# Weight splits one per slot, input rows split in two portions, sample values and large copies asked for at other times

## The reference

```
u = rmsnorm(x) @ w_in                       # 1024 -> 10256 columns
o_a, state = gla(q, k, v, log_a, state0)    # gated linear attention, 4 heads
for window, dilation in ((128, 1), (512, 4), (2048, 16)):
    o_g, lse_g, new_cache_g = dilated_attention(q_g, k_g, v_g)
o_b = softmax(lse) weighted sum of o_g
merged = sigmoid(ga) * ((norm(o_a) * silu(gg)) @ w_gla_branch) + sigmoid(gb) * ((o_b * silu(dg)) @ w_dil_branch)
h = x + rmsnorm(merged @ w_out)
y = h + (pe @ w_ple_proj) * sigmoid(h @ w_ple_gate)
```

## Time and profile before

| | us |
|---|---|
| median of 3 runs | 2909.12 (2906.79 to 2913.81) |
| the profiled execution | 2904.35 |
| its span | 2902.2 |
| PE busy | 2659.9 (92%) |
| DVE, ACT, POOL busy | 1673.6, 1031.6, 806.6 |
| granted clock of PE, mean | 0.962 |

### The profile page before, as it was taken

One profiled execution on the slowest core, in us unless ns is written; L12 is line 12 of the kernel. 1 busy time (PEld: TensorE's weight loads), 2 busy tenths in 40 slices (PEclk: granted clock), 3 DMA queues, 4 the chain that ended last, 5 costly groups with the idle time before them and its releaser, 6 DMA issues. The chain is left out here.

```text
span 2902.2 us, 54195 instructions
## 1 busy us (share of the span) xinstructions
PE 2659.9 (92%) x21916; PEld 2045.2 (70%) x21916; DVE 1673.6 (58%) x3025; ACT 1031.6 (36%) x1880; POOL 806.6 (28%) x805
## 2 busy tenths in 40 slices
PE   4778989998979999899999987999999999999998
PEld 3667867776867778788998886997887544444444
DVE  6455766654544565556666654667655565554552
ACT  4222544322211222223334443544433344444441
POOL 5234322432333444333325322332222000000000
PEclk8899999999989999999999998999999999999999
DMA  5588766978787788768758676544435976666552
GB/s 155 124 255 276 262 220 219 326 261 275 245 266 243 247 246 299 276 225 287 239 174 295 212 247 235 186 155 140 139 133 201 316 198 157 173 168 165 167 115 56
DMA packets 370057, 622.38 MB, mean 214 GB/s; under 512 B 199196, under 2 KB 204899, under 8 KB 365330
## 3 DMA queue, kind: packets, MB, share of 16 engines
q1 hardware_dynamic: 311554, 352.11, 39.3%
q0 software_dynamic: 44000, 233.26, 24.4%
q10 hardware_dynamic: 14256, 33.56, 3.2%
HBM read 429.15 MB, written 244.66 MB: 232 GB/s over the span
## 5 line engine op out<-in xcount | busy, mean ns | idle before, releaser
L832 PE MATMUL out<-w_hi,x_hi 128*128 128x256 f16 x3136 | 868.3, 277 | 52.8 <-DVE stage L750 28.6
L832 PE MATMUL out<-w_lo,x_hi 128*128 128x256 f16 x3136 | 867.6, 277 | 0.0
L832 PE MATMUL out<-w_hi,x_lo 128*128 128x256 f16 x3136 | 867.0, 276 | 0.0
L750 DVE SCALAR_TENSOR_TENSOR stage<-out,stage 128x512 f32<-128x512 f32 (+1 forms) x567 | 378.5, 680 | 408.8 <-PE out L832 291.7
L684 DVE SCALAR_TENSOR_TENSOR w_lo<-raw,w_hi 128x1024 f16<-128x1024 f32 x280 | 403.2, 1455 | 19.0 <-ACT w_hi L680 18.4
L830 PE MATMUL out<-x_hi,w_hi 128*128 128x256 f16 x1344 | 372.8, 277 | 31.0 <-ACT stage L738 13.9
L680 ACT ACTIVATE w_hi<-raw 128x1024 f16<-128x1024 f32 x280 | 285.3, 1049 | 318.5 <-POOL raw L699 118.6
L832 PEld LDWEIGHTS out<-w_hi,x_hi 128*128 128x128 f16 x3136 | 311.7, 99 | 104.9 <-issue 30.4
L830 PE MATMUL out<-x_hi,w_lo 128*128 128x256 f16 x1344 | 372.5, 277 | 0.0
L830 PE MATMUL out<-x_lo,w_hi 128*128 128x256 f16 x1344 | 372.4, 277 | 0.0
L832 PEld LDWEIGHTS out<-w_hi,x_lo 128*128 128x128 f16 x3136 | 311.6, 99 | 41.6 <-issue 1.3
(11 more groups left out here) (351 smaller groups left out, 4575.3 us busy)
## 6 DMA issues: line engine op xcount, KB each, us to landing
raw<-in_w_in SPq DMA_DIRECT2D x80, 1024.0 KB, 10.7
out<-in_cache_kv_w POOLq DMA_DIRECT2D x64, 1020.0 KB, 9.0
U<-stage SPq DMA_DIRECT2D x224, 256.0 KB, 4.1
UT<-stage SPq DMA_DIRECT2D x96, 256.0 KB, 6.4
sw_kc<-in_cache_kv_w ACTq DMA_DIRECT2D x24, 1024.0 KB, 10.2
sw_vc<-in_cache_kv_w POOLq DMA_DIRECT2D x24, 1024.0 KB, 9.8
sw_rows<-U POOLq DMA_DIRECT2D x32, 512.0 KB, 7.4
out<-in_cache_kv_w POOLq DMA_DIRECT2D x16, 1008.0 KB, 6.7
```

What stands on the lines that cost most here:

```text
L750: return dve.scalar_tensor_tensor(out=out, in0=self.shaped(D, self.product(D, f, us), us), scalar=1.0 / W_SCALE, in1=other, op0=ALU.mult, ...
L832: return pe.matmul(out, x[:, 2 * d + u, f * HALF_K + k, :], w[:, k, :], start=start, stop=stop)
```

## The change

Weights: `HI_AT` and `LO_AT` are now the same in both phases, with one form in a slot and the lo part one slot after the hi part; the sums have slots of their own; raw weights are loaded at the third and fourth slot of a generation; semaphore counts follow the new order of forms (`cut_count`). The sample step of D = 1 comes after four forms instead of two. Input rows: two spare buffers, lent from `stage1`, let tiles 6 and 7 be loaded at the start; the splits are made in two portions, in two slots; the first portion waits for no sums; norms, scales and splits of pairs 2 to 4 are one to three slots earlier; pairs 5 to 8 start at slot 16 every 11 slots. The values of the first sample are loaded 13 slots earlier. The copies of `keep_rows` go to slots 425 and 430, 500 and 510, 640 and 660 (before 420, 480, 540). In the cutter loads come two slots later, and DVE's part and the store one slot later. Nothing else in what is computed changes. Changed lines only:

```diff
-SUM_AT = (1, 1)
-HI_AT = ((3, 6, 6, 7, 9, 10, 10), (2, 5, 5, 6, 8, 9, 10))
-LO_AT = ((4, 7, 7, 8, 10, 11, 12), (3, 6, 6, 7, 9, 10, 11))
-RAW_PARTS = ((2, 4), (1, 2))
+SUM_AT = {P7: 1, P6: 5, P4: 7, P5: 8}
+HI_AT = {P1: 4, P2: 5, P7: 6, P6: 7, P4: 9, P5: 10, P3: 11}
+LO_AT = {f: at + 1 for f, at in HI_AT.items()}
+NEXT_SUM = {P1: P6, P2: P4, P7: P5}
+RAW_PARTS = ((3, 4), (3, 4))
...
+def cut_count(G, f):
+    order = list(HI_AT) if G else list(range(FORMS))
+    return FORMS * G + order.index(f) + 1
...
-        order.insert(2, (SAMPLE_STEP, (0,)))
+        order.insert(2 if D > 1 else 4, (SAMPLE_STEP, (0,)))
...
+KEEP_SLOTS = ((425, 430), (500, 510), (640, 660))
...
-    FIRST_SLOT, EVERY = 14, 9
-    def __init__(self, bind, bank, x_prompt, x_sample, g_pre, identity, xf, xs, XB):
+    FIRST_SLOT, EVERY = 16, 11
+    def __init__(self, bind, bank, x_prompt, x_sample, g_pre, identity, xf, xs, XB, spare):
...
-        self.x = [sb(f"x{s}", [P, D_MODEL]) for s in range(self.RING)]
+        self.x = [sb(f"x{s}", [P, D_MODEL]) for s in range(self.RING)] + spare
...
+    def buffer(self, i):
+        if self.RING <= i < len(self.x):
+            return i, 0
+        turn = i if i < self.RING else i - (len(self.x) - self.RING)
+        return turn % self.RING, turn // self.RING
...
-        return self.x[i % self.RING][:self.rows(i), :]
+        return self.x[self.buffer(i)[0]][:self.rows(i), :]
...
-            eng.wait_ge(self.row_lo, k - self.BY_TENSOR + 1)
+            eng.wait_ge(self.row_lo, 2 * (k - self.BY_TENSOR + 1))
...
-        if i >= self.RING:
-            self.wait_used(sp, self.owner(i - self.RING))
+        s, turn = self.buffer(i)
+        if turn > 0:
+            before = max(j for j in range(i) if self.buffer(j)[0] == s)
+            self.wait_used(sp, self.owner(before))
...
-        sp.dma_start(self.tile(i), src).then_inc(self.x_loaded[i % self.RING], 16)
+        sp.dma_start(self.tile(i), src).then_inc(self.x_loaded[min(s, self.RING)], 16)
...
-    def split_hi(self, act, k):
+    def part_of(self, moves, part):
+        middle = len(moves) // 2
+        return moves[:middle] if part == 0 else moves[middle:]
+    def split_hi(self, act, k, part):
+        s = self.row_set(k)
...
-        act.wait_ge(self.summed, self.sums_before(k + 1))
-        s = self.row_set(k)
-        before = [j for j in range(self.BY_TENSOR, k) if self.row_set(j) == s]
-        if before:
-            self.wait_turned(act, before[-1])
-        for dst, src in self.moves(k, self.row[s][0]):
+        if part == 1:
+            act.wait_ge(self.summed, self.sums_before(k + 1))
+        else:
+            before = [j for j in range(self.BY_TENSOR, k) if self.row_set(j) == s]
+            if before:
+                self.wait_turned(act, before[-1])
+        for dst, src in self.part_of(self.moves(k, self.row[s][0]), part):
...
-    def split_lo(self, dve, k):
-        dve.wait_ge(self.row_hi, k - self.BY_TENSOR + 1)
+    def split_lo(self, dve, k, part):
...
-        his = [dst for dst, _ in self.moves(k, self.row[s][0])]
-        for (dst, src), hi in zip(self.moves(k, self.row[s][1]), his):
+        dve.wait_ge(self.row_hi, 2 * (k - self.BY_TENSOR) + part + 1)
+        his = [dst for dst, _ in self.part_of(self.moves(k, self.row[s][0]), part)]
+        for (dst, src), hi in zip(self.part_of(self.moves(k, self.row[s][1]), part), his):
...
-        sp.wait_ge(self.row_lo, k - self.BY_TENSOR + 1)
+        sp.wait_ge(self.row_lo, 2 * (k - self.BY_TENSOR + 1))
...
-        if slot in (3, 7):
-            for i in ((6, 7) if slot == 3 else (8,)):
+        if slot == 0:
+            for i in self.tiles(3):
...
-        for k, at in ((2, 4), (3, 6), (self.SAMPLE, 9)):
-            if slot == at:
-                self.split_hi(act, k)
+        if slot == 4:
+            self.square(act, self.tiles(self.SAMPLE)[0])
+        for k, at in ((2, 1), (3, 4), (self.SAMPLE, 8)):
+            if slot in (at, at + 1):
+                self.split_hi(act, k, slot - at)
...
-            if slot == self.base(k) + 2:
-                self.split_hi(act, k)
+            if slot in (self.base(k) + 3, self.base(k) + 4):
+                self.split_hi(act, k, slot - self.base(k) - 3)
...
-        if slot == 4:
+        if slot == 1:
...
-        if slot == 8:
+        if slot == 6:
...
-        for k, at in ((2, 5), (3, 7), (self.SAMPLE, 10)):
-            if slot == at:
-                self.split_lo(dve, k)
+        for k, at in ((2, 2), (3, 5), (self.SAMPLE, 9)):
+            if slot in (at, at + 1):
+                self.split_lo(dve, k, slot - at)
...
-            if slot == self.base(k):
-                for i in self.tiles(k):
-                    self.scale(dve, i)
-            if slot == self.base(k) + 3:
-                self.split_lo(dve, k)
+            if slot in (self.base(k), self.base(k) + 1):
+                self.scale(dve, self.tiles(k)[slot - self.base(k)])
+            if slot in (self.base(k) + 4, self.base(k) + 5):
+                self.split_lo(dve, k, slot - self.base(k) - 4)
...
+            if slot == self.base(k) + 1:
...
-        if slot == 0:
-            for i in (6, 7):
-                self.load(sp, i)
-        if slot == 5:
+        if slot == 3:
...
-        for k, at in ((2, 6), (3, 8), (self.SAMPLE, 11)):
+        for k, at in ((2, 4), (3, 7), (self.SAMPLE, 11)):
...
-            if slot == self.base(k) + 4:
+            if slot == self.base(k) + 6:
...
-            if slot == self.base(k) + 7:
+            if slot == self.base(k) + 9:
...
-            eng.wait_ge(self.lo_ready, FORMS * G + P1 + 1)
+            eng.wait_ge(self.lo_ready, cut_count(G, P1))
...
-            eng.wait_ge(self.lo_ready, FORMS * G + P2 + 1)
+            eng.wait_ge(self.lo_ready, cut_count(G, P2))
...
-            eng.wait_ge(self.lo_ready, FORMS * G + P7 + 1)
+            eng.wait_ge(self.lo_ready, cut_count(G, P7))
...
-        for H, phase, at in self.coming(q):
+        for H, _, at in self.coming(q):
...
-                if at == HI_AT[phase][f]:
+                if at == HI_AT[f]:
...
-        for H, phase, at in self.coming(q):
+        for H, _, at in self.coming(q):
...
-                if at == LO_AT[phase][f]:
+                if at == LO_AT[f]:
...
-        for H, phase, at in self.coming(q):
-            if at == SUM_AT[phase]:
-                self.sum(pool, H, P7)
-            for f, lower in ((P6, P1), (P4, P2), (P5, P7)):
-                if at == LO_AT[phase][lower]:
+        for H, _, at in self.coming(q):
+            for f in (P7, P6, P4, P5):
+                if at == SUM_AT[f]:
...
-        pe.wait_ge(self.lo_ready, FORMS * G + f + 1)
+        pe.wait_ge(self.lo_ready, cut_count(G, f))
...
+        if r == -11:
+            self.load_v(q, 0)
...
-                if c == 0:
-                    self.load_v(q, 0)
...
-        i = self.at(r + CUT_PERIOD + 3)
+        i = self.at(r + CUT_PERIOD + 1)
...
-        i = self.at(r - 1)
+        i = self.at(r - 2)
...
-        i = self.at(r)
+        i = self.at(r - 1)
...
-            inputs = Inputs((early, sem), side, a["x_prompt"], a["x_sample"], a["g_pre"], identity, xf, xs, XB)
+            spare = [stage[1][:, 2 * i:2 * i + 2, :].rearrange("p a c -> p (a c)") for i in range(2)]
+            inputs = Inputs((early, sem), side, a["x_prompt"], a["x_sample"], a["g_pre"], identity, xf, xs, XB, spare)
...
-            for i in range(2, inputs.RING):
+            for i in range(2, 2 * PAIRS):
...
-            def keep_rows(g):
-                window = kv_prompt[g].shape[2]
-                for part, column in ((0, U_DK), (1, U_DV)):
-                    cols = slice(column + g * WIDTH, column + (g + 1) * WIDTH)
-                    if g > 0 or part > 0:
-                        pool.dma_start(kv_prompt[g][0, 0, :, part].rearrange("l h d -> l (h d)"), U[SEQ - window:SEQ, cols]).then_inc(copied, 16)
-                    pool.dma_start(kv_sample[g][0, :, window - DEC_SEQ:window, part].rearrange("b l h d -> b l (h d)"),
-                                   U[SEQ:TOKENS, cols].rearrange("(b l) c -> b l c", b=DEC_BATCH)).then_inc(copied, 16)
+            def keep_rows(g, part):
+                window, column = kv_prompt[g].shape[2], (U_DK, U_DV)[part]
+                cols = slice(column + g * WIDTH, column + (g + 1) * WIDTH)
+                if g > 0 or part > 0:
+                    pool.dma_start(kv_prompt[g][0, 0, :, part].rearrange("l h d -> l (h d)"), U[SEQ - window:SEQ, cols]).then_inc(copied, 16)
+                pool.dma_start(kv_sample[g][0, :, window - DEC_SEQ:window, part].rearrange("b l h d -> b l (h d)"),
+                               U[SEQ:TOKENS, cols].rearrange("(b l) c -> b l c", b=DEC_BATCH)).then_inc(copied, 16)
...
-                    if q == gen_slot(COLUMN_TILES + 3 * (g + 1) + 1):
-                        projection.wait_tiles(pool, COLUMN_TILES + 3 * (g + 1))
-                        projection.wait_samples(pool, COLUMN_TILES)
-                        keep_rows(g)
```

(5 more changed lines are left out.)

19 lines of the change are left out of this document (10 added, 9 removed).

## The result

Both kernels on one chip, four runs each: the changed kernel takes 2874.02 us (2871.72 to 2879.16), the kernel before 2911.47 (2906.79 to 2916.71). The ratio is 0.9873, with a 95% interval of 0.985 to 0.9896. That is 37 us faster. The forecast was 2836, a gain of 73: the sign and the range hold, the size is half. The profiled execution has a span of 2869.6 us against 2902.2, 32.6 less.

The account below looks back on a forecast made before the run. PE's own work plus 242 us idle and low clock were taken to bound the kernel. 8 + 14 + 4 + 3 + 16 + 31 − 3 + 0 = 73 us gained gave 2836 us, range 2808 to 2880.

Parts of the forecast that it names:

- Start: 0 to 100 us: later sample step and earlier transposes together gain 8 us (bounds 4 and 12).
- the second effect: Start of the kernel: the chain making the transposes starts earlier, so pair 3 lands sooner; gain 0 to 4 us.
- Input pairs: 100 to 300 us: wider spacing gains 14 us of idle time (4 to 24) and 4 of clock (0 to 8).
- that wait shrinks: Input pairs: ACT's 14.48 us wait for rows of x shrinks without vanishing; half of 28.1 us idle taken, 14.
- Rival (c): Start and input pairs give nothing, DVE's new stop and SP's queued transposes using up the saving; price 26 us, chance 10%.
- Weights, first phase with the cutter: 300 to 800 us: evacuations wait for one lo part, not two, against later cutter stores; +3 us (−15 to +15).
- Weights, second phase: Second phase: smaller evacuation waits against weight loads asked for one to two slots later; 0 us (−10 to +10).
- Rival (d): Weight order makes P6 late in each of 38 column tiles; at 2.3 us each it costs 87, 2923; chance 3%.
- Sample values: First sample's attention: value loads 13 slots earlier cut DVE's 18.64 us wait to 0 to 4; gain 16 (6 to 22).
- rival (b): Value loads only change place: weights of 819 come 8 to 16 us later, PE stops for P6; price 16, chance 8%.
- Large copies: Window 2's two 4 MB copies no longer precede the keys: gain 31 us (25 to 33), less 3 at the GLA.
- Rival (a): Large copies only change place: DVE waits twice for the GLA's queries; price 24 us more, 2860, chance 7%.

Follow-up runs that it names:

- row_loads_sooner: The changed kernel with the later pairs' loads of x asked for two slots earlier, ahead of the transposes on SP: 2868.58 us, ratio 0.9856.
- weights_back: The changed kernel with the splitting of the weights (slots, order, subtractions, weight loads) as before: 2841.48 us, ratio 0.9765.
- raw_back: The changed kernel with the second phase's weight loads asked for in the places of before: 2866.78 us, ratio 0.9857.
- p6_third: The changed kernel with P6's hi and lo parts one slot earlier, third among the parts, and P7's one later: 2863.59 us, ratio 0.9843.
- weights_cutter_back: The changed kernel with the weights' places and the cutter's load, DVE part and store as before: 2863.57 us, ratio 0.9837.
- per_phase: The changed kernel with weight tables by phase: the first with P6's parts third, the second as before: 2823.5 us, ratio 0.9703.
- caches_later: per_phase with cache copies beginning at half tile 12 instead of 3, the 18 displaced ones made from half tile 62 to 70: 2810.92 us, ratio 0.9672.
- loads_eight: per_phase with the later pairs' loads of x four slots earlier, eight slots ahead of a pair's base: 2819.67 us, ratio 0.9699.
- p1_sooner: per_phase with the changed kernel's second-phase weight places, except P1's hi part at slot 2 and P6's subtraction at 3: 2821.67 us, ratio 0.9725.

## Why the prediction was right in part

**Start: right in sum.** Forecast 8, measured 8.5 at column tile 1. The new stop of PE near 46 is there (5.87 us at 52.88), and it cost nothing. The 7.24 us of the earlier trace rows are gone; what is left is one wait of 12.1 us for `x_lo<-row1l`, against 6.7 and 6.6 for pairs 2 and 3 before. It ends at 84.98, where the last such wait before ended at 85.25. So the second effect, the earlier chain (0 to 4), gave 0.3, and nearly all of the 8.5 comes from the place of the sample step (5 to 7).

**Input pairs: wrong.** Forecast 14 + 4; measured a lead that falls from 8.5 to 1.4, and to −0.1 with weights and cutter put back. So it is −7 to −8 where +18 was said, an error of 25. The step that failed was "that wait shrinks", taken as half of the idle time. ACT's waits for rows of x, of which the earlier trace rows is one, did not shrink (40.4 us in 6 before, 43.5 in 7 in the changed kernel), and where row_loads_sooner made them vanish most of the lead was lost two tiles later. The earlier trace rows had a hint, a DMA share of 0.76 over 200 us, which in the kernel before runs from 0.67 to 1.03 in the slices of 25 us from 125 on. Rival (c) named the loss of both terms, and its price of 26 is nearly what tile 5 lacks (1.4 against 8 + 18), but it put it down to a chain in SP's queue. What the runs showed in its place is the cache copies, 12 of them and 11 of the 46 MB moved there: nothing waits for them, and without them 15.5 us of lead stay.

**Weights, first phase with the cutter: right in sum, wrong in each piece.** Forecast +3 (−15 to 15). The weights' places netted −1 by tile 22 (31.3 against 32.4 with them back); their "at least 2 slots" of room for P6 were not there, in 12 tiles of the first phase. The step "DVE's cut is one slot later too, so DVE sees no difference" was false: the cutter's move gave 21 us, and DVE's waits for it fell by 32. The row that it needed, DVE's 98.9 us of waits for `cut_hi`, was not among those read; the earlier trace rows gives ACT's side only, and its waits for the store did not grow (151.9 us before, 140.1 in the changed kernel).

**Weights, second phase: wrong.** Forecast 0 (−10 to 10), measured −31 by weights_back. The failing step is "weight loads are asked for one to two slots later": it looked at the loads, which cost nothing that could be told (raw_back), and passed over P1, which went from slot 2 to 4 there and from 3 to 4 in the first phase. The slots were counted for PE's own use of the parts. They were not counted for the side work on the other engines: on POOL a subtraction waits for P1's lo part in front of the side work's loads. That place is 9 to 13 us of it; how P1's slot costs the rest stays open.

**Rival (d): its mechanism, not its price.** P6's wait for `w_lo` came in 14 of 39 column tiles, 54.7 us, not 2.3 us in each. It decided nothing by itself, because PE waited 40 us less for evacuations in the first phase. A chance of 3% was too low for it; p6_third's lead of 52 at tile 17, against 34, is what it cost there.

**Sample values: near.** Forecast 16. In weights_cutter_back, where nothing else moves there, the lead goes from 0.2 (tile 12) by −7.3 (tile 14) to 11.2 (tile 17): a price of 7 before the sample and a gain of 18 in it. The wait of the earlier trace rows is 1.35 us now. The price of 0 to 5 was too low, and rival (b) had its first half: the weights for which POOL waits until 819.19 in the earlier trace rows came 6 us later. But PE did not stop for P6. ACT has the hi parts made from them in front of its copies of the sample's transposed keys, `sw_kT`, and PE waited for those 7.1 us, where it was 1.5 before. The timelines of POOL, ACT and PE in weights_cutter_back:

```profile
825.29 2.34 POOL L713 TENSOR_TENSOR raw<-raw 128x1024 f32<-128x1024 f32 x1 [22.30 <-DMA raw<-in_w_in]
830.15 2.95 ACT L702 ACTIVATE w_hi<-raw 128x1024 f16<-128x1024 f32 x3 [14.68 <-POOL raw L717]
833.72 1.94 PE L2068 MATMUL out<-identity,sw_kc 128*128 128x128 f32 x8 [7.14 <-ACT sw_kT L2126]
```

Of the Trainium skill's rule (DMA: Bandwidth & Descriptors, Queues, rings and completion order), by which the weights would lose only their share: the 6 us against the 10.3 of one common line lies between, and doesn't decide it.

**Large copies: right.** Forecast 31 − 3, measured 29 at tile 31 and 32 to 35 in the whole. The −3 was not due: per_phase has no loss at the GLA with the copies in the same place. Rival (a) falls.

In sum, with the places that the ledger gives: 8.5 − 7 (pairs) + 18.5 (to tile 12, most of it the cutter) + 14 (tiles 12 to 17) − 3 − 20 (windows) + 29 − 10 + 3 (after tile 39) = 33, the difference of the spans. Two terms make the miss: the input pairs, −7 for +18, and the weights in the second phase, −30 (windows and GLA) for 0. The cutter, which the forecast had at nothing, gave some 20 back and hid a part of it.

## What to carry to other kernels

When a step is moved by a slot, count the room not only for its user but for every queue in which something waits for it: here one form's parts and one subtraction on POOL, two slots later, cost 31 to 49 us, of which loads held up behind that subtraction were only 9 to 13. Where a stretch doesn't gain by spacing its steps, look for transfers in it that nobody waits for: here 18 copies of up to 1 MB, moved away, were worth 15 us in the traces and 9 by the ratios. And compare traces by the start of the same instruction, column tile by column tile: the total hid a loss of 31 under a gain of 21 and one of 32.

## What the runs showed of the hardware

- The time of a DMA transpose depends on what goes beside it: the same transpose of a pair's rows took 4.2 to 5.0 us in caches_later and 20.57 in loads_eight, where the DMA share was 1.27 with cache copies under way. A high share alone doesn't do it: in the kernel before, the two at 200 took 4.99 and 4.30 at 1.03.
- DVE's scaling of x, 1.28 us in most rows, took 3.37 where POOL's subtraction ran beside it, and that, begun beside the DVE instruction ahead, took 3.25 in place of 2.35:

```profile
229.85 1.21 DVE L707 SCALAR_TENSOR_TENSOR w_lo<-raw,w_hi 128x1024 f16<-128x1024 f32 x1
230.99 3.37 DVE L442 SCALAR_TENSOR_TENSOR x<-x,rstd,g 128x1024 f32<-128x1024 f32 x1
```
```profile
230.02 3.25 POOL L725 TENSOR_TENSOR raw<-raw 128x1024 f32<-128x1024 f32 x1
```

  The tables decide how often the two meet. Of the 280 lo parts on DVE, 69 before and 119 in the changed kernel overlap an operation of POOL by more than 0.1 us; those take 2.18 and 2.27 us in the mean, all others 1.22. So the mean of all 280 goes from 1455 ns to 1663, with the same instructions: 61 us of the 69 that the page shows DVE to be busier. It is 1567 in p6_third and 1487 in p1_sooner. The Trainium skill (SBUF — State Buffer, Who interferes with whom) says that a DVE instruction with two SBUF inputs contends with a GpSimd instruction that reads SBUF. The rows agree: POOL's is 0.9 longer and overlaps DVE's lo part by 1.0, DVE's scaling is 2.1 longer and overlaps POOL's by 2.3.
